# Running sums laid over all partitions: read back from device memory by DMA, or made by selector products on TensorE

## The reference, cut to what matters

```
def ssd_scan(xh, a, bg, cg, chunk):
    ...
    a_cum = jnp.cumsum(a, axis=2)
    seg = a_cum[:, :, :, None] - a_cum[:, :, None, :]
    mask = jnp.tril(jnp.ones((chunk, chunk), dtype=bool))[:, :, None, None]
    decay = jnp.exp(jnp.where(mask, seg, -jnp.inf))
    scores = jnp.einsum('bclgn,bcsgn->bclsg', cm, bm)
    y_diag = jnp.einsum('bclsg,bclsgr,bcsgrp->bclgrp', scores, decay, x)
    ...
y_f = direction(xs, bm, cm, dt_f, dt_bias_f, a_log_f)
y_b = flip(direction(flip(xs), flip(bm), flip(cm), flip(dt_b), dt_bias_b, a_log_b))
```

## Time and profile before

| | |
|---|---|
| runs of before | 1673.35 us median (1672.75 to 1674.73) |
| profiled execution | 1672.55 us, span 1670.7 us |
| TensorE products busy | 1653.4 us (99%) |
| weight loads of TensorE busy | 1379.2 us (83%) |
| VectorE busy | 1004.7 us (60%) |
| ScalarE busy | 847.4 us (51%) |
| GpSimd busy | 62.8 us (4%) |
| moved by DMA | 303.73 MB, 182 GB/s |

### The profile page before, as it was taken

One profiled execution on the slowest core, in us unless ns is written; L12 is line 12 of the kernel. 1 busy time (PEld: TensorE's weight loads), 2 busy tenths in 40 slices (PEclk: granted clock), 3 DMA queues, 4 the chain that ended last, 5 costly groups with the idle time before them and its releaser, 6 DMA issues.

```text
span 1670.7 us, 19678 instructions
## 1 busy us (share of the span) xinstructions
PE 1653.4 (99%) x7734; PEld 1379.2 (83%) x7734; DVE 1004.7 (60%) x1246; ACT 847.4 (51%) x1197; POOL 62.8 (4%) x59
## 2 busy tenths in 40 slices
PE   7999999999999999999999999999999999999998
PEld 6888888888888888888888888888888888888886
DVE  5876677776666677766565554444444445454454
ACT  5666566666565444544445454444544444335543
POOL 0000000000000233000000000000000000000000
PEclk9999999999999999999999999999999999999999
DMA  8555565655656664445565666566666665666563
GB/s 239 172 162 157 176 172 170 173 172 147 187 178 185 197 186 155 146 141 178 186 234 178 219 189 187 190 191 189 183 193 192 190 188 187 191 195 183 181 198 135
DMA packets 198462, 303.73 MB, mean 182 GB/s; under 512 B 14577, under 2 KB 70497, under 8 KB 198241
## 3 DMA queue, kind: packets, MB, share of 16 engines
q1 hardware_dynamic: 198048, 302.00, 59.9%
q10 hardware_dynamic: 320, 0.47, 0.1%
HBM read 300.33 MB, written 2.10 MB: 181 GB/s over the span
## 4 chain that ended last, share of the span: by engine, by line
PE 94%; DVE 2%; issue 1%; DMA 1%; ACT 1%; SPq 1%; POOL 0%; POOLq 0%; DVEq 0%; ACTq 0%
PE G L1259 29%; PE G L1261 29%; PE G L1260 29%; PE S L1267 2%; PE S L1390 1%; DVE wlo L734 1%; DMA raw<-in_w_in 0%; PE S L1377 0%; PE S L1395 0%; PE S L1383 0%; PE S L1259 0%; PE S L1260 0%; PE S L1261 0%; PE S L1354 0%; PE S L1433 0%
## 5 line engine op out<-in xcount | busy, mean ns | idle before, releaser
L449 ACT ACTIVATE whi<-raw 128x1024 fp32r<-128x1024 f32 x556 | 588.7, 1059 | 742.9 <-PE G L1261 712.6
L734 DVE TENSOR_TENSOR wlo<-raw,whi 128x1024 fp32r<-128x1024 f32 x556 | 676.7, 1225 | 424.5 <-ACT whi L449 424.2
L1259 PE MATMUL G<-whi,a_hi 128*128 128x512 f32 x1472 | 581.3, 395 | 2.0 <-DVE wlo L734 1.2
L1261 PE MATMUL G<-whi,a_lo 128*128 128x512 f32 x1472 | 574.0, 390 | 0.0
L1260 PE MATMUL G<-wlo,a_hi 128*128 128x512 f32 x1472 | 573.6, 390 | 0.0
L1259 PEld LDWEIGHTS G<-whi,a_hi 128*128 128x128 f32 x1472 | 276.8, 188 | 59.3 <-issue 2.0
L1261 PEld LDWEIGHTS G<-whi,a_lo 128*128 128x128 f32 x1472 | 276.7, 188 | 58.4
L1260 PEld LDWEIGHTS G<-wlo,a_hi 128*128 128x128 f32 x1472 | 277.0, 188 | 55.6
L1259 PE MATMUL G<-whi,b_hi 128*128 128x512 f32 x752 | 293.8, 391 | 0.0
L1260 PE MATMUL G<-wlo,b_hi 128*128 128x512 f32 x752 | 293.0, 390 | 0.0
L1261 PE MATMUL G<-whi,b_lo 128*128 128x512 f32 x752 | 292.9, 390 | 0.0
(11 more groups left out here) (185 smaller groups left out, 859.2 us busy)
## 6 DMA issues: line engine op xcount, KB each, us to landing
raw<-in_w_in SPq DMA_DIRECT2D x136, 512.0 KB, 3.8
raw<-in_w_mlp_in SPq DMA_DIRECT2D x128, 512.0 KB, 4.2
raw<-in_w_mlp_out SPq DMA_DIRECT2D x128, 512.0 KB, 4.2
raw<-in_w_in SPq DMA_DIRECT2D x72, 256.0 KB, 3.5
raw<-in_w_in SPq DMA_DIRECT2D x144, 128.0 KB, 3.6
raw<-in_w_ssm_up SPq DMA_DIRECT2D x32, 512.0 KB, 3.8
raw<-in_w_attn_up SPq DMA_DIRECT2D x32, 512.0 KB, 3.8
raw<-in_w_out SPq DMA_DIRECT2D x32, 512.0 KB, 4.3
```

The costliest lines, as they stand in the source:

```text
L449: act.activation((whi_end if end else whi)[:, slot, 0:width], raw[:, slot, 0:width], ACT.Copy).then_inc(hi_made, 1)
L734: dve.tensor_tensor((wlo_end if end else wlo)[:, slot, 0:width], raw[:, slot, 0:width], (whi_end if end else whi)[:, slot, 0:width].bitcas ...
L1259: pe.matmul(out_ap, hi[:, k, cols], w_hi, start=start, stop=False)
L1261: return pe.matmul(out_ap, lo[:, k, cols], w_hi, start=False, stop=stop)
```

## The change

The running sums go to a scratch of 64 KB in device memory, `cum_rows`, and from there, per group and pair of heads, to all 128 partitions by a DMA with a repeated source. The products L1377, the `pick` matrices, the constant `sel` and the remainders go away; `avx` and the rows of `cum` are half as many. ScalarE's queue issues one store of 64 KB and 16 loads of 512 KB each (two per group: 128 partitions by two directions by two heads by 256 tokens). The first pair is issued in `decays` at p = 7, behind a wait for the store; each further pair in `conv` of its group at p = 1. `ex` is made from `segs` in SBUF in place of `S`. The transposes of `conv` wait for `tm_made` in place of `seg_made`.

```
-    pick = place("pick", [P, 2, 4, P], F32R)
+    segs = place("segs", [P, 2, 2, 2, T])
...
+    cum_rows = nc.dram_tensor("cum_rows", (2, HEADS, T), F32).ap()
...
                 act.wait_ge(dt_mm, 2)
-                act.activation(cum[:, :], S[:, 2, 0:T], ACT.Copy).then_inc(c_made, 1)
+                act.activation(cum[0:DTW, :], S[0:DTW, 2, 0:T], ACT.Copy).then_inc(c_made, 1)
+                act.wait_ge(c_made, 2)
+                act.dma_start(cum_rows.rearrange("d h t -> (d h) t"), cum[0:DTW, :]).then_inc(s_cum, 16)
+            if p == 7:
+                act.wait_ge(s_cum, 16)
+                act.wait_ge(sq_x, TB)
+                load_segs(0)
+
+        def load_segs(g):
+
+            for half in range(2):
+                rows = cum_rows[:, 4 * g + 2 * half:4 * g + 2 * half + 2, :]
+                act.dma_start(segs[:, half, :, :, :], rows.unsqueeze(0).to_broadcast([P, 2, 2, T])
+                              ).then_inc(s_segs[half], 16)
...
+            if p == 1 and not first(g):
+                act.wait_ge(seg_made, 2 * g)
+                load_segs(g)
             if p == 3:
...
-                act.activation(pick[:, :, :, :], sel[:, :, ds(g * 4, 4)].unsqueeze(3).to_broadcast([P, 2, 4, P]),
-                               ACT.Copy).then_inc(pick_made, 1)
                 masked_dt(g, (0,))
...
-                act.wait_ge(fb_mm, 2 * g + (half + 1))
+                act.wait_ge(s_segs[half], 16 * (g + 1))
...
                         last = act.activation(ex[:, 2 * half + h, c * P:(c + 1) * P],
-                                              S[:, 0, h * T + c * P:h * T + (c + 1) * P], ACT.Identity, bias=minus)
+                                              segs[:, half, 0, h, c * P:(c + 1) * P], ACT.Identity, bias=minus)
...
-                dve.wait_ge(c_made, 2)
-                dve.tensor_tensor(cum[DTW:P, :], S[DTW:P, 2, 0:T], cum[DTW:P, :].bitcast(F32), ALU.subtract
-                                  ).then_inc(c_made, 1)
...
-                        last = dve.scalar_tensor_tensor(out=part, in0=S[:, 1, h * T + c * P:h * T + (c + 1) * P],
+                        last = dve.scalar_tensor_tensor(out=part, in0=segs[:, half, 1, h, c * P:(c + 1) * P],
...
                     for d in range(2):
-                        last = pe.matmul(S[:, 2, c * P:(c + 1) * P],
-                                         avx[:, c, d, :, :, :].rearrange("p a b h -> p (a b h)"), masks[:, 2 + d, :],
+                        last = pe.matmul(S[0:DTW, 2, c * P:(c + 1) * P],
+                                         avx[:, c, d, :, :].rearrange("p a h -> p (a h)"), masks[:, 2 + d, :],
                                          start=(d == 0), stop=(d == 1))
...
                 if not first(g):
-                    pe.wait_ge(seg_made, 2 * g)
+                    pe.wait_ge(tm_made, 2 * g)
...
         def scan(p, g, pr, pp):
-            if p in (1, 3):
-                half = p // 2
-                if half:
-                    pe.wait_ge(seg_made, 2 * g + 1)
-                else:
-                    pe.wait_ge(tm_made, 2 * g + 2)
-                    pe.wait_ge(pick_made, g + 1)
-                    if first(g):
-                        pe.wait_ge(c_made, 3)
-                for d in range(2):
-                    for h in range(2):
-                        last = pe.matmul(S[:, d, h * T:(h + 1) * T], pick[:, d, 2 * half + h, :], cum[:, :],
-                                         start=True, stop=True)
-                last.then_inc(fb_mm, 1)
             if p == 3:
                 pe.wait_ge(scan_v, g * SCAN_V + 3)
```

More of the change, by code:

```diff
@@ L218, in build @@
     masks = place("masks", [P, 4, P])
-    sel = place("sel", [P, 2, HEADS])
     cs = place("cs", [P, 4, T])
@@ L234, in build @@
     av = place("av", [P, TB, 2, HEADS])
-    avx = place("avx", [P, TB, 2, 2, 2, HEADS])
-    cum = place("cum", [P, T], F32R)
+    avx = place("avx", [P, TB, 2, 2, HEADS])
+    cum = place("cum", [P, T])
     neg_cum = place("neg_cum", [P, TB, 2, HEADS])
@@ L294, in build @@
     st_mm, st_made, y_mm, off_mm = sem("st_mm"), sem("st_made"), sem("y_mm"), sem("off_mm")
-    pick_made, fb_mm, f_made, seg_made = sem("pick_made"), sem("fb_mm"), sem("f_made"), sem("seg_made")
+    s_cum, s_segs = sem("s_cum"), [sem("s_segs0"), sem("s_segs1")]
+    f_made, seg_made = sem("f_made"), sem("seg_made")
     c_made, set_rope = sem("c_made"), sem("set_rope")
@@ L366, in scan_parameters @@
             sp.dma_start(masks[:, :, :].rearrange("p m n -> p (m n)"), consts[:, P:5 * P]).then_inc(s_masks, 16)
-            sp.dma_start(sel[:, :, :].rearrange("p d h -> p (d h)"), consts[:, 9 * P:9 * P + DTW]
-                         ).then_inc(s_masks, 16)
         def rope_parameters():
@@ L530, in conv @@
                                    ).then_inc(cv_made, 1)
+            if p == 1 and not first(g):
+                act.wait_ge(seg_made, 2 * g)
+                load_segs(g)
             if p == 3:
                 if first(g):
-                    act.wait_ge(s_masks, 32)
+                    act.wait_ge(s_masks, 16)
                     act.wait_ge(dt_v, 18)
@@ L759, in _ @@
         dve.memset(cv[:, :, half + T:2 * half + T], 0.0).then_inc(set_cv, 1)
-        dve.memset(avx[:, :, :, :, :, :].rearrange("p c d a b h -> p (c d a b h)"), 0.0).then_inc(set_cv, 1)
+        dve.memset(avx[:, :, :, :, :].rearrange("p c d a h -> p (c d a h)"), 0.0).then_inc(set_cv, 1)
         dve.wait_ge(rows_t, 1)
@@ L864, in decays @@
                     for d in range(2):
-                        dve.tensor_copy(avx[:, c, d, :, d, :], av[:, c, d, :].unsqueeze(1).to_broadcast([P, 2, HEADS])
-                                        ).then_inc(dt_v, 1)
+                        dve.tensor_copy(avx[:, c, d, d, :], av[:, c, d, :]).then_inc(dt_v, 1)
             if p == 6:
-                dve.wait_ge(c_made, 2)
-                dve.tensor_tensor(cum[DTW:P, :], S[DTW:P, 2, 0:T], cum[DTW:P, :].bitcast(F32), ALU.subtract
-                                  ).then_inc(c_made, 1)
                 dve.wait_ge(dt_dec, 1)
@@ L1326, in decays @@
                 pe.wait_ge(dt_v, DT_A)
-                pe.wait_ge(s_masks, 32)
+                pe.wait_ge(s_masks, 16)
                 pe.wait_ge(set_up, 6)
@@ L1356, in conv @@
                 if first(g):
-                    pe.wait_ge(c_made, 3)
+                    pe.wait_ge(c_made, 2)
                 else:
@@ L1537, in shape_constants @@
         parts += [table[:P], table[P:]]
-    parts.append(t % DTW == np.arange(DTW)[None, :])
     return np.concatenate([np.asarray(a, np.float32) for a in parts], axis=1)
```

## The result

The changed kernel takes 1664.94 us (median of 5 runs, 1664.76 to 1666.24), the kernel before in the same session 1673.35 us (median of 5, 1671.67 to 1674.73). The ratio is 0.995, with a 95% interval of 0.9939 to 0.996: faster by 0.5%, or 8.4 us between the medians. The forecast was 1665.9 us with a range of 1663 to 1669.5. The profiled execution went from 1672.55 to 1664.94 us, 7.6 us less.

A forecast was written before the change was run, and what follows sets the result against it. TensorE's gapless stream was taken to bound the kernel. Removing the selector products saves 7.4 us and all other terms count 0: 1673.35 - 7.4 = 1665.9 us against the median, range 1663 to 1669.5 us.

The forecast's parts named there:

- The bound: Whole kernel: TensorE's gapless stream plus what happens before 70 us sets the time; TensorE waits for nobody in the scan.
- The products, 7.4 us: Scan windows: removing 64 selector products saves 0.93 us per group, 7.4 us in 8 groups.
- `avx`, 0: Four products of `decays` with 64 columns instead of 128: gain taken as 0, at most 0.5 us.
- The low end of the range: 1663 us: 0.5 us of `avx`, runs 0.6 us under the median, about 2 us for small things ahead of 70 us.
- ScalarE's queue, 0: `conv` of groups 1 to 7: issuing two loads takes 0.74 us and fits in ScalarE's 1.66 us wait, costing 0.
- Rival B: ScalarE held at the pair's issue in 7 `conv`: TensorE waits 7.3 us each, 51 us, 1717 us; chance 0.05.
- The DMA engines, 0: A pair takes 3.9 us of all 16 engines, idle 4.6 us between 151 and 159.5 us; cost 0.
- the idle hole: DMA engines between 151 and 159.5 us: idle for 4.6 us, which a pair of 3.9 us nearly fills.
- The turn-taking of the queues: Loads on ScalarE's queue take turns with weights, holding them up by up to 3.9 us, still covered.
- The first group: Store, wait and first pair from 65.6 us: cost 0 under some 5.9 us of lead, upper end a few us.
- Rival A: A wait in the first group takes part of the gain once: TensorE waits 3.6 us, 1669.5 us; chance 0.05.
- Rival C: Reading the same 4 KB on all engines is slow and delays weights behind it: 1670.2 us; chance 0.06.

The follow-up runs named there:

- the run with eight copies: Changed kernel with eight idle 128x512 copies on ScalarE behind the pair's issue in `conv` of groups 1 to 7: 1680.79 us, ratio to before 1.0053.
- the runs at 2 and 5.3 us: Changed kernel with three or eight idle ScalarE copies behind the pair's issue in `conv` of groups 1 to 7: 1665.02 us and 1680.79 us.

## Why the prediction was right, point by point

**The bound.** Right: TensorE's stream is the time. Its busy time fell by 1653.4 - 1646.7 = 6.7 us and the span by 7.6 us.

**The products, 7.4 us.** Right, a little low. Each group is 0.95 us shorter, not 0.93: the six distances from group 1 to group 7 add up to 300.52 us before and 294.80 us now. That 8 x 0.95 = 7.6 us is just the difference of the two profiled executions is partly chance. The distance of groups 0 and 1, which holds `decays`, shrank by 0.76 us only (54.23 to 53.47), and the transposes of group 0 began 0.14 us earlier, by no more than such starts differ between runs. The missing 0.02 us lies behind the selector products: at p = 1 of group 2 the last product of one piece and of the next triple were 1.16 us apart before and 0.68 us now, 0.48 us instead of 0.46. I had read only to the first product after the four; the next few start some 0.01 us late each. The distances show the products; the run with only the loads and the one without them show that the transfers are not in the sum. The rest of the change (`pick`, remainders, the reads of `ex`) was not run alone, but between 70 and 460 us TensorE waits for nothing in either trace. The medians of the first session differ by 8.4 us, of which 0.8 us is that the profiled execution of before was under its median; later sessions put before at 1672.3 and 1672.6 us, 7 to 8 us above the versions with the same stream.

**`avx`, 0.** Right: in the changed kernel the eight entries of these products fill 1.02 us of the stream (63.11 to 64.13 us), before 0.89 us (63.20 to 64.09). Half the columns saved nothing and may have cost 0.1 us.

**The low end of the range.** One reading behind it was wrong. I put nearly all of TensorE's 17.3 idle us ahead of 70 us. Before, the rows ahead of 70 us and behind 1640 us are

```profile
0.00:70.00 70.00, 60.78 (x298) 50.04 (x299) 47.25 (x98) 41.54 (x71) 1.02 (x6) 1.00 0.71 209
1640.00:1670.70 30.70, 22.86 (x100) 18.42 (x99) 14.04 (x20) 9.74 (x15) 1.10 (x2) 0.94 0.30 113
```

so 9.2 us are idle ahead of 70 us and 7.8 us behind 1640. The forecast does not use this; only some 2 us of the range do.

**ScalarE's queue, 0.** Right in the result and too careful in the working. I put the issue, 0.74 us, into the idle time behind the piece; it runs beside the ACTIVATE instead. Rival B did not occur, since the issue took 0.89 us for the pair. Its price was nearly right: the run with eight copies gives 2.3 us per group for a delay that I priced at 1.9. B put its turning point at 4.3 us for the pair; the runs at 2 and 5.3 us lie on its two sides. The delay there came from copies and not from an issue.

**The DMA engines, 0.** Right that they are hidden, but two things were off. The cost: 3.9 us per pair was worked out from weight loads. Measured by the queue's share it is 27 / 7 = 3.8 us, so the figure was good, but by luck: the same bytes from distinct rows take 18 / 7 = 2.6 us, and it is the repeated source, which the working left out, that brings them back to 3.8. And the reason: I made the idle hole carry the argument. The pair at the fullest place cost nothing either, so there TensorE's lead did it alone. Doubling shows that the two together have an end: with two pairs at p = 1 TensorE begins to wait. What the hole adds to the lead was not measured, since no run doubles the pair at the full place.

**The turn-taking of the queues.** The Trainium skill, "DMA: Bandwidth & Descriptors", section "Queues, rings and completion order", says that an engine takes turns between the queues that have work for it, a packet at a time. I took from it that loads on ScalarE's queue would hold up weights already under way. The runs agree: in the median of seven groups 7.0 us with the pair on the other queue, 4.9 with it behind in the same one, 4.6 with none. The rule alone does not explain the groups in which the load was late with the pair behind it in its own queue, up to 6.3 us; that stays open. The delay from the other queue, 1.6 to 3.0 us, lies under the 3.9 that I allowed.

**The first group.** Right. The store landed after 3.5 us, at the short end of the bounds of 3.4 to 8.4, and the piece that I saw at 70.5 us began at 70.19. The Trainium skill, "DMA: Bandwidth & Descriptors", section "Anatomy of one DMA — SWDGE (gpsimd) path", says of DMAs on GpSimd's path that the receipt from the memory written makes most of the fixed time and can be long for device memory. This store went out on ScalarE's queue, and no long receipt shows: it landed after 3.1 to 4.1 us in the nine profiles that have it, and loads of 64 KB into SBUF in the changed kernel took 3.4 to 4.1 us. The first half's rows were read at 77.48 us without a wait. Rival A did not occur.

**Rival C** was half a true story: a repeated source does take longer (7.9 us against 6.1), but the weight beside it was late by 1.6 to 3.0 us, not by the 8.4 that it needed.

## What to carry to other kernels

When one engine's stream has no gaps, what an instruction costs is the distance between the starts around it, read a few instructions further than the one that follows. A transfer that replaces it is free as long as the chain behind each late weight stays ahead of that engine; adding the transfers alone, removing them alone, and doubling them tells in three runs whether they are free and how near the limit is. If a bulk load must not hold up the one ahead of it, try it behind that load in the same queue: here that cut the delay of the load ahead from 2.4 to 0.3 us in the median, though the time of the kernel stayed the same.

## What the runs showed of the hardware that I had not expected

- A load that repeats 4 KB of device memory over 128 partitions took the DMA engines longer than one of distinct rows of the same size and shape: 1.6 against 1.1% of the span for 7.34 MB in the changed kernel, 1.25% when each pair was doubled. It landed after 7.9 against 6.1 us in the median.
- A DMA on ScalarE's queue was issued while an ACTIVATE of the same engine was running (148.32 and 148.29 us).
- Behind a pair that repeats its source SP's issues take long, behind one of distinct rows they do not. With the pair under way the two loads that SP issued at 151.05 us took 3.33 us to issue (first fence below), and 3.57 us with the pair on SP's own queue. With as many bytes of distinct rows in flight the same two took 0.98 us (second fence), as at this place of the kernel before. Over groups 1 to 7 it is 0.98 to 1.17 us with distinct rows and 2.4 to 3.6 us in the changed kernel. So here the number of bytes queued is not the cause; what about the repeated source is, no run shows. SP had time for it. ScalarE's own queue was slowed only when the pairs were doubled: the second pair took 1.73 us to issue in place of 0.89 (third fence).

```profile
150.64 0.37 SPq L410 DMA_DIRECT2D raw<-in_w_in  x1
151.05 3.33 SPq L413 DMA_DIRECT2D raw<-in_w_in  x2
```

```profile
149.97 0.37 SPq L412 DMA_DIRECT2D raw<-in_w_in  x1
150.38 0.98 SPq L415 DMA_DIRECT2D raw<-in_w_in  x2
```

```profile
149.67 1.73 ACTq L552 DMA_DIRECT2D spare<-cum_rows  x2
```

- Reading `ex` from SBUF in place of the banks made neither engine faster: ScalarE 387 ns in place of 364, VectorE 346 in place of 344.
